# A hybrid attention and short-convolution layer on eight cores: halo columns inside the convolution matmuls, and the adaLN gate summed on VectorE

## What is computed

```python
shift, scale, gate = split(silu(c) @ w_mod + b_mod, 3)            # (B, 2048) each
h  = rms_norm(x, norm_g) * (1 + scale) + shift                    # (B, 4096, 2048)
q, k, v, ga, b, cg, hh, gc = split_proj(h @ w_in)
attn = silu(ga) * latent_attention(rope(q), rope(k), v, kc, vc)
u    = cg * hh                                                    # (B, L, 1024)
conv = silu(gc) * (b * (u[-1] * w0 + u[0] * w1 + u[+1] * w2))     # neighbours in position
x    = rms_norm(x + gate * (concat(attn, conv) @ w_out), final_norm_g)
```

## Time and profile before

| | |
|---|---|
| median of 3 runs | 1103.71 us |
| profiled execution, its own time | 1102.39 us |
| its span (slowest core, core 6) | 1100.9 us |
| spans of the eight cores | 1089.1 to 1100.9 us |
| mean granted TensorE clock of the cores | 0.963 to 0.970 |
| TensorE, VectorE, ScalarE busy | 929.0, 343.5, 456.5 us |

### The profile page before, as it was taken

How to read it: one execution, slowest core, us unless ns; L and a number is a source line. 1 busy time by engine, 2 the same in 40 slices (tenths; PEclk the granted TensorE clock), 3 DMA queues, 4 the chain that set the end, 5 groups by cost and what they waited for, 6 DMA issues and landing times.

```text
span 1100.9 us, 17627 instructions; the slowest of 8 cores (1089.1 to 1100.9 us)
## 1 busy us (share of the span) xinstructions
PE 929.0 (84%) x6932; PEld 520.8 (47%) x6932; DVE 343.5 (31%) x623; ACT 456.5 (41%) x706; POOL 57.7 (5%) x59
## 2 busy tenths in 40 slices
PE   0009994884799879999999999999999998999995
PEld 0006552542444434444444444656666655565542
DVE  1001211263568465422111222010011233333287
ACT  0001110244556635100000002998988777777300
POOL 1000003200000000011111111000000000000000
PEclk9999996988799989999999999999999999999998
DMA  8999999429443535666655321960002020201311
GB/s 134 169 170 171 168 171 214 115 77 209 135 78 78 114 81 153 113 115 116 115 104 96 70 39 48 168 130 1 2 1 78 1 78 1 78 21 58 154 72 81
DMA packets 12001, 109.40 MB, mean 99 GB/s; under 512 B 1296, under 2 KB 1296, under 8 KB 5008
## 3 DMA queue, kind: packets, MB, share of 16 engines
q0 software_dynamic: 5616, 73.40, 38.2%
q1 hardware_dynamic: 6304, 34.87, 8.7%
HBM read 173.28 MB, written 8.39 MB: 165 GB/s over the span
## 4 chain that ended last, share of the span: by engine, by line
PE 68%; DMA 15%; DVE 8%; issue 4%; ACT 4%; DVEq 0%; POOL 0%; ACTq 0%; POOLq 0%; SPq 0%
PE PS L173 67%; DMA wst<-w_mod 7%; DMA xb<-xT 4%; DMA x<-xq 2%; DVE on L208 1%; DMA tabk<-tab 1%; DVE xo L195 1%; ACT PT L192 1%; DVE ytmp L195 1%; ACT hT L192 1%; PE PS L176 1%; DVE kraw L195 1%; ACT kraw L192 1%; DVE x L195 1%; DVE xo L208 1%
## 5 line engine op out<-in xcount | busy, mean ns | idle before, releaser
L192 ACT ACTIVATE PT<-PS,smx 128x1024 bf16<-128x1024 f32 x272 | 288.5, 1114 | 56.6 <-PE PS L173 56.4
L173 PE MATMUL PS<-hT,wcv 128*128 128x512 bf16 x1024 | 228.9, 378 | 0.0
L173 PEld LDWEIGHTS PS<-V,PT 128*128 128x128 bf16 x2176 | 146.8, 98 | 62.1 <-issue 2.2
L173 PE MATMUL PS<-V,PT 128*128 128x130 bf16 x2176 | 169.3, 221 | 0.4 <-ACT PT L192 0.4
L173 PE MATMUL PS<-qT,KT 128*128 128x512 bf16 x544 | 162.7, 381 | 2.7 <-ACT PT L192 2.5
L173 PEld LDWEIGHTS PS<-hT,wcv 128*128 128x128 bf16 x1024 | 98.4, 97 | 117.5
L173 PE MATMUL PS<-wkv,xb 128*128 128x512 bf16 x384 | 85.2, 383 | 0.0
L173 PE MATMUL PS<-s_bf,wst 128*128 128x2 bf16 x512 | 14.5, 164 | 83.1 <-DMA wst<-w_mod 83.1
L173 PE MATMUL PS<-wo,mixC 128*128 128x512 bf16 x256 | 68.7, 381 | 1.4 <-DVE ytmp L195 0.2
L173 PE MATMUL PS<-wo,mixA 128*128 128x512 bf16 x256 | 68.3, 379 | 0.0
L173 PEld LDWEIGHTS PS<-qT,KT 128*128 128x128 bf16 x544 | 44.4, 97 | 46.2 <-issue 4.3
(11 more groups left out here) (124 smaller groups left out, 856.7 us busy)
## 6 DMA issues: line engine op xcount, KB each, us to landing
wst<-w_mod POOLq DMA_DIRECT2D x8, 2048.0 KB, 34.1
wcv<-w_conv POOLq DMA_DIRECT2D x8, 2048.0 KB, 15.9
xb<-xT POOLq DMA_DIRECT2D x6, 2048.0 KB, 49.5
x<-xq SPq DMA_DIRECT2D x4, 2048.0 KB, 23.9
wgt<-w_gate POOLq DMA_DIRECT2D x8, 1024.0 KB, 17.7
wo<-w_out POOLq DMA_DIRECT2D x4, 2048.0 KB, 36.2
xo<-xown SPq DMA_DIRECT2D x8, 1024.0 KB, 5.2
out<-xo SPq DMA_DIRECT2D x16, 512.0 KB, 2.7
```

The lines of the kernel that those rows point to most:

```text
L173: self.op("tensor", lambda e: e.matmul(out, lhsT, rhs, start=start, stop=stop), [out], [lhsT, rhs], signal)
L192: self.op("scalar", lambda e: e.activation(out=out, in_=in_, func=func, **kw), outs, ins)
```

## The change

- hT becomes one buffer of 16 rows x 1026 columns; the two halo tokens are copied to columns 1024 and 1025 after `kv_quarter(1)`. Slots 6 to 8 move up by 64 bytes to make room.
- Groups 1 and 2 of a convolution tile are multiplied in three pieces of 342 columns (`conv_mm`); the matmuls of 2 columns are gone. The halo products are the last two columns of the third piece.
- The gate: `sbc` is gone. `gate_sum(i)`, on VectorE at the end of tile i, sums wgt times silu(c) over the 16 rows kc into `gacc` (float32) and splits it into two bf16 halves `ghl`. `gate_put(i)`, at the head of the next tile, sums over partitions with two ones-matmuls of 256 columns.
- The next wgt is loaded once gate_sum has read the last.

```diff
-    hT = [at(f"hT{i}", [128, 16, 512], BF16, SL[4 + i]) for i in range(2)]
+    hT = at("hT", [128, 16, OWN + 2], BF16, SL[4])
...
+        if i == 1:
+            P.copy(hT[:, :, OWN:OWN + 2], hH[:])
...
+    def gate_sum(i):
+
+        for kc in range(KC):
+            if kc == 0:
+                P.ts(V_, gacc[:], wgt[:, kc, :], s_f[:, kc, 0:1], ALU.mult)
+            else:
+                P.stt(gacc[:], wgt[:, kc, :], s_f[:, kc, 0:1], gacc[:], ALU.mult, ALU.add)
+        if i < 7:
+            load("wgt", wgt, dr["w_gate"][i + 1])
+        P.copy(ghl[0][:], gacc[:])
+        P.tt(V_, ghl[1][:], gacc[:], ghl[0][:], ALU.subtract)
+
+    def gate_put(i):
+        for j in range(2):
+            P.mm(bank(7, 256), ones_bf[:], ghl[j][:], j == 0, j == 1, j == 1)
+        gs = gate_bc[:, i * 256:i * 256 + 256]
+        P.tt(V_, gs, bank(7, 256), gs, ALU.add)
+
+    def conv_mm(w, g, c0, n):
+        b = next_bank()
+        for kc in range(KC):
+            P.mm(bank(b, n), w[:, kc, g, :], hT[:, kc, c0:c0 + n], kc == 0, kc == KC - 1, kc == KC - 1)
+        return b
+
     for i in range(8):
         w = wcv[i % 3]
         if i > 0:
-            gate_mm = i - 1
-            for kc in range(KC):
-                P.mm(bank(7, 256), sbc[:, kc, :], wgt[:, kc, :], kc == 0, kc == KC - 1, kc == KC - 1)
...
+            gate_put(i - 1)
+        for j in range(3):
+            b = conv_mm(w, 1, 342 * j, 342)
+            P.act(cg_sb[:, 342 * j:342 * j + 342], bank(b, 342), AF.Copy)
...
+        for tt in range(2):
+            b = conv_mm(w, 0, 512 * tt, 512)
+            s0 = slice(tt * 512, tt * 512 + 512)
+            P.tt(V_, acc2[:, s0], bank(b), acc_c[:, s0], ALU.mult)
+        for tt in range(2):
+            b = conv_mm(w, 3, 512 * tt, 512)
+            P.act(sgc[:, tt * 512:tt * 512 + 512], bank(b), AF.Silu)
+        gate_sum(i)
```

More of the change, by code:

```diff
@@ L279, in body @@
     zeros_bf = fixed("zeros_bf", [128, 128], BF16)
-    sbc = fixed("sbc", [128, 16, 128], BF16)
+    s_f = fixed("s_f", [128, 16, 2])
+    gacc = fixed("gacc", [128, 256])
+    ghl = [fixed(f"ghl{i}", [128, 256], BF16) for i in range(2)]
     s_bf = fixed("s_bf", [128, 16, 2], BF16)
@@ L297, in body @@
     slot0 = (cur[0] + 63) // 64 * 64
-    SL = [slot0 + 16384 * i for i in range(9)]
+    SL = [slot0 + 16384 * i + (64 if i > 5 else 0) for i in range(9)]
     work0 = SL[8] + 16384
@@ L377, in body @@
     P.memset(V[:, :, :, 128:130], 1.0)
-    P.act(s_bf[:].rearrange("p k r -> p (k r)"), cc_sb, AF.Silu)
+    P.act(s_f[:].rearrange("p k r -> p (k r)"), cc_sb, AF.Silu)
+    P.copy(s_bf[:], s_f[:])
     P.op(V_, lambda e: e.reduce_max(out=smx[:, 0:1], in_=qg_sb, axis=AX.X, apply_absolute_value=True),
@@ L384, in body @@
     P.copy(ident_bf[:], ident_f)
-    P.copy(sbc[:], s_bf[:, :, 0:1].broadcast_to([128, 16, 128]))
     def mod_tile(t, c0, b):
@@ L525, in hq @@
         q = i - 1
-        return hT[q // 2][:, :, (q % 2) * 256:(q % 2) * 256 + 256]
+        return hT[:, :, q * 256:q * 256 + 256]
     def rstd_mm(h, b):
@@ L569, in kv_quarter @@
             blk = (i - 1) % 2 * 2 + j
-            kv_own(hT[t - 6][:], blk, kraw[t][:], blk, 2 + 4 * t + blk)
+            kv_own(hT[:], 4 * (t - 6) + blk, kraw[t][:], blk, 2 + 4 * t + blk)
+        if i == 1:
+            P.copy(hT[:, :, OWN:OWN + 2], hH[:])
     def halo():
@@ L641, in q_step @@
         b = (0, 1, 2, 3)[i % 4]
-        h = hT[blk // 4]
         for kc in range(KC):
-            P.mm(bank(b), h[:, kc, (blk % 4) * 128:(blk % 4) * 128 + 128], wq[half][:, kc, :], kc == 0, kc == KC - 1,
+            P.mm(bank(b), hT[:, kc, blk * 128:blk * 128 + 128], wq[half][:, kc, :], kc == 0, kc == KC - 1,
                  kc == KC - 1)
@@ L697, in ga_step @@
         for kc in range(KC):
-            P.mm(bank(b), w[:, kc, (h % 4) * 128:(h % 4) * 128 + 128], hT[tt][:, kc, :], kc == 0, kc == KC - 1,
-                 kc == KC - 1)
+            P.mm(bank(b), w[:, kc, (h % 4) * 128:(h % 4) * 128 + 128], hT[:, kc, tt * 512:tt * 512 + 512], kc == 0,
+                 kc == KC - 1, kc == KC - 1)
         P.act(sga[tt][:, h, :], bank(b), AF.Silu)
@@ new lines, in body @@
+            gate_put(i - 1)
+        for j in range(3):
+            b = conv_mm(w, 1, 342 * j, 342)
+            P.act(cg_sb[:, 342 * j:342 * j + 342], bank(b, 342), AF.Copy)
+        if i == 0:
+            k_put(rotk[1], 4, CTX + 7 * 512, 7)
+        for j in range(3):
+            b = conv_mm(w, 2, 342 * j, 342)
+            n = 342 if j < 2 else 340
+            P.tt(V_, u_sb[:, 1 + 342 * j:1 + 342 * j + n], bank(b, n), cg_sb[:, 342 * j:342 * j + n], ALU.mult)
+        ends = u_sb[:, 0:1026:1025]
@@ new lines, in body @@
+        P.tt(V_, ends, bank(b)[:, 340:342], cg_sb[:, OWN:OWN + 2], ALU.mult)
+        P.tt(V_, ends, ends, hmask_sb, ALU.mult)
+        cw = convw_sb[:, i * 3:i * 3 + 3]
+        P.ts(V_, acc_c[:], u_sb[:, 1:1025], cw[:, 1:2], ALU.mult)
+        P.stt(acc_c[:], u_sb[:, 0:1024], cw[:, 0:1], acc_c[:], ALU.mult, ALU.add)
+        P.stt(acc_c[:], u_sb[:, 2:1026], cw[:, 2:3], acc_c[:], ALU.mult, ALU.add)
+        for tt in range(2):
+            b = conv_mm(w, 0, 512 * tt, 512)
+            s0 = slice(tt * 512, tt * 512 + 512)
+            P.tt(V_, acc2[:, s0], bank(b), acc_c[:, s0], ALU.mult)
@@ L767, in body @@
         load(f"wo{c}", wo[c], dr["w_out"][c])
[L768 to L771, removed]
+    gate_put(7)
     P.dma("sync", "fg", fg_sb[:], dr["fg"])
```

## The result

The changed kernel takes 1142.55 us, median of 4 runs (1141.84 to 1148.15); the kernel before took 1104.18 on the same chip (1103.5 to 1106.93). The ratio is 1.0355 [1.0323, 1.0386]: **slower by 3.5%**, 38.4 us, where 34.7 were forecast. The profiled execution is the longest of the four, 1148.15 us, 5.6 above its median; its spans are compared with that in mind.

What follows compares the result with a forecast made beforehand. TensorE alone was taken to bound the convolution: each of 8 tiles saves 2.23 us, waits 4.1 and loses 2.1 to the clock, 31.8 in all; with 2.9 in the own-token stage, +34.7 us, 1138 us, range 1118 to 1148.

Steps and rivals of the forecast that it cites:

- Unit costs of matmuls: Convolution tile on TensorE: 342-column matmuls at 0.145 us save 0.70, the gate saves 1.53; 2.23 us less a tile.
- VectorE's chain: gate_sum at a tile's end: 10.1 us until TensorE against 5.95 available, so TensorE waits about 4.1 us a tile.
- The clock: After each tile's wait TensorE's granted clock falls, costing 2.1 us a tile, bounds 1.3 and 2.9.
- A: Rival: pauses stay just short of lowering the clock; +17.9 us, 1121 us; chance 0.12.
- The last tile: Its wait stands before attention's first score matmuls, priced like the other tiles; POOL's later final product was put at nothing.
- The own stage: Own-token stage before the q projection: quarters of hT sharing 32-byte cells wait for each other; +2.9 us, bounds 1.4 and 5.
- The first wait: Own-token stage: the fourth quarter's squares on ScalarE wait for VectorE's writes of the third; +1.42 us.
- the stop for the fourth quarter: Own-token stage: block 5's projection waits row by row for the fourth quarter's writes; q projection begins 2.9 us later.
- the bound of 5: Upper bound in us for the own-token stage's loss, if the clock falls while the matmuls trickle.
- B: Rival: dependence between VectorE operations costs nothing, wait 2.4 us without a clock fall; +4.3 us, 1108 us; chance 0.07.
- C: Rival: bf16 weights make multiply-adds 0.35 us and dependence is free; -11.7 us, 1092 us; chance 0.05.
- D: Rival: clock recovers late in each tile and own stage costs 5 us; +43, 1147 us; inside the forecast's 0.72.

Runs made afterwards that it cites:

- the version that keeps the savings: Changed kernel with gate_put behind group 1 of the next tile, hT rows padded to 1040, last gate_put eight steps into attention: 1086.82 us, ratio 0.9828.
- filling: Changed kernel with 32 useless 256-column matmuls ahead of the ones-matmuls in seven tiles, covering TensorE's pause: 1153.52 us on a slower chip, ratio 1.018.
- the gate part alone: Kernel before with only the gate changed, keeping two hT buffers and the 2-column halo matmuls: 1144.74 us, ratio 1.0341.
- Padding: Changed kernel with hT's rows padded from 1026 to 1040 elements so that quarters share no 32-byte cell: 1142.06 us, ratio 1.0329.
- the first fill: Changed kernel with 16 useless 256-column matmuls ahead of the ones-matmuls in seven tiles: 1138.63 us, ratio 1.0292.
- two running sums: Changed kernel with gate_sum alternating between two running sums that are added at the end: 1119.09 us, ratio 1.011.

## Why the prediction was right

**Direction and size.** 38.4 us slower by the runs, 34.7 forecast, time inside the range and within 5 us of the number.

- **Unit costs of matmuls**: -0.70 for the 342-column pieces, measured -0.68; -2.23 in all, measured 30.18 - 27.97 = 2.21 (27.97 is a tile of the version that keeps the savings). The price between the 256 and the 512 columns held.
- **VectorE's chain**: 10.1 us forecast up to TensorE, 10.25 measured. A multiply-add is 0.484 busy, so a 256-element row of another operand mix was the right price; multiply 0.344, cast 0.294, subtraction 0.426. They start 0.588 apart, not 0.581: 8.83 for 15 where the sum has 8.72. (That the row of 15 also reads 8.72 is chance, for it ends with the last one's end and leaves out the last gap.) Against the longer chain stands that the first matmul of the pair waits for the cast alone and is done inside the wait, which the prediction did not see. The two small errors nearly cancel: the pause of 3.52, the 0.16 by which the busy time of the last matmul ahead of it reaches into the pause, and 0.43 more between the pair are 4.11, forecast 4.1.
- **The clock**: 2.1 taken, 1.98 measured by filling, as a mean; single tiles cost from nothing (the one of core 3) to 2.8. What was said of when it falls does not hold: 1.78 us lowered it in 36 of 48 tiles, and 3.52 us left it up in one. With pauses shorter by half, A would still not have been the result.
- **The last tile was mis-sized.** The prediction put POOL's `mixC` at nothing ("the product is read in the next tile's group 0"). In the last tile, which has no loads behind `gate_sum`, it stretches the chain by 1.9 us (5.42 against 3.52). Convolution and attention together grow by 30.95 + 3.64 = 34.6 us where 31.8 were forecast: 2.8 short. The last tile's pause gives 1.9 of it, the clock of seven tiles takes 0.8 back, and the rest lies in attention, +3.64 where one fall of 2.1 was forecast. It is not pinned down: in kernels that end this stage in the same way attention takes from 418.75 (the gate part alone) to 421.52.
- **The own stage was mis-sized.** +2.9 taken, +3.96 measured. The first wait is 1.37 (1.42 forecast) and the stop for the fourth quarter is there, but behind it 47 matmuls take 11.99 us where 47 x 0.216 = 10.2 is full speed. The granted clock is 0.67 from 306.00 to 309.40: it falls, as the bound of 5 assumed. Padding takes 3.6 of it back.
- **Not forecast**: +1.05 between q projection and convolution. Nothing on the change's path runs there, and the other kernels lie between 129.7 and 131.1, one at 133.5, against 130.31. It is left open.

By stage the terms that the change owns come to 34.6 + 3.96 = 38.6, against 34.7; the runs say 38.4. So close an agreement is partly luck: the two profiled executions themselves differ by 45.8, and what is left out of the sum is 4.66 and 1.05 without a tested cause.

**The rivals.** A (1121) fell by the windows at 0.50 and with the first fill. B (1108) fell by 0.588 against 0.396: dependence costs 0.19 us an operation. The Trainium skill's rule (VectorE: DVE Perf Modes, "The DRAIN you can't avoid") that a semaphore after each operation costs nothing extra does not carry over to this chain, where each operation waits for the sum just written; the 8 copies behind that rule are not said to read one another's result. C (1092) needs 0.43 a step, and 0.588 is measured: the bfloat16 weights do not shorten the operation, 0.48 busy. Steps that do not depend on one another are 0.396 apart, under the 0.43, so the dependence decided against C. D (1147) was right on the own stage's lower clock and on single tiles: core 7's first period is 34.74.

## What to carry to other kernels

Work moved off the bound engine pays only if its result is not asked for at the next instruction: find the slack between the last input and the consumer and compare it with the whole dependent chain on the other engine, start to start. Moving the consumer by one group turned 3.5% slower into 0.5% faster, and with the last pair moved too and padded rows it is 1.7% faster, with not one operation less. A pause on TensorE costs about one and a half times its length here, 4.1 us and 2.0 behind it. Before joining two buffers, look at whether their parts still end where the dependency tracker can tell them apart.

## What was not expected of the hardware

**POOL's product holds VectorE up.** While POOL multiplies two SBUF tensors (2.35 to 2.52 us), a VectorE operation that reads two SBUF tensors does not get done until POOL is: 2374 ns instead of 485, 2.83 us instead of 0.43. It is not so for VectorE operations that read one of the two from PSUM: in the trace of before `gate_bc`, PSUM and SBUF, runs at its 0.42 us inside POOL's product, in all 64 cases (8 tiles, 8 cores):

```profile
500.12 2.36 POOL L195 TENSOR_TENSOR mixC<-acc,sgc 128x1024 bf16<-128x1024 f32 x1
500.82 0.42 DVE L195 TENSOR_TENSOR gate_bc<-PS,gate_bc 128x256 f32<-128x256 f32 x1 [7.96 <-PE PS L173]
```

The Trainium skill (SBUF — State Buffer, "SBUF: two separate sides") states just this: a pair of ports is locked by a VectorE operation with two SBUF inputs or by GpSimd for the whole instruction, and the other is blocked. The rows agree on who is blocked, and applied to the last tile it gives what the prediction lacked there. The section also says that whichever starts first gets the pair; the subtraction of 2.83 us starts 0.18 before POOL's product by the profile (623.62, 623.80) and is still the one that waits. POOL's times are rough, so this stays open. Each of these places was seen with POOL's product 128 x 1024 only, and that VectorE holds POOL up is not shown here.

**The clock falls after shorter pauses than rows of before let one think**: 1.78 us idle ahead of the pair was enough in 36 of 48 tiles, 2.82 was not at one place of before, 3.52 was not in one tile of the changed kernel, and 1.03 in the first five tiles of two running sums was not. What decides between them, beside the length, was not tried.
